# A two-block transformer kernel on one core: VectorE's list in the block-wise inverse, with the work between two levels placed behind the next level's copy

## The chip, the core and the metric

The program runs on one core of a Trainium2 chip. A core has TensorE (matmuls, PE in the profile), VectorE (DVE), ScalarE (ACT), GpSimd (POOL) and SyncE (SP), which issues most of the DMAs. Each engine works through its own list of instructions in the order in which they stand there; they meet only at semaphores. The metric is the device time of one execution, in microseconds (us); lower is better.

## The reference

`first_block` feeds `second_block`. The change lies in the first block's token mixers, in the gated delta rule. For each of 4 tiles of 128 tokens and both directions the kernel needs the inverse of a unit lower triangular matrix of each of 4 heads, and then it carries a state over the tiles:

```python
decay = jnp.exp(jnp.where(incl, gc[..., :, None] - gc[..., None, :], -jnp.inf))
lower = jnp.where(strict, jnp.einsum('bnhid,bnhjd->bnhij', kb, kc) * decay, 0.0)
t_inv = lax.linalg.triangular_solve(eye + lower, ...)
...
def step(s, xs):
    v_new = u_i - jnp.einsum('bhcd,bhde->bhce', w_i, s)
    o_i = ... + jnp.einsum('bhcj,bhje->bhce', qk_i, v_new)
    s = s * gl_i[..., None, None] + jnp.einsum('bhcd,bhce->bhde', kd_i, v_new)
```

Beside it the block computes a neighbourhood attention (softmax over 512 keys, with a bias), a differential attention, a Fourier mix, an output projection, and an expert-choice feed-forward with 16 experts. The second block is another mixer with another set of experts. Everything is float32.

## The kernel before

The whole program is written out by hand: each engine has one function in which every instruction and every semaphore wait stands in the order in which it is to run. Nothing is scheduled by a tool.

**The inverse.** The 4 token tiles (`t` = 0 to 3) follow one another; each takes 6 levels (`lv` = 1 to 6), which double the size of the inverted diagonal blocks. A level is written below as (t, lv). It is a loop over two engines:

1. TensorE, `solve_left` (L1752; at level 6 half the size, L1757): y = lower x inverse, 32 small matmuls.
2. VectorE, the copy of y with a mask into `turned` (L2999; at level 6 L3001).
3. TensorE, `solve_right`: the product p (L1776, at level 6 L1770) and its twin pd (L1783), 32 matmuls each, which read the copy.
4. VectorE, the subtraction of p from `invT` (L3006) and of pd from `inv` (L3011). The next level's `solve_left` reads `invT`, so it waits for the first of the two.

**What is laid between.** Level number n (0 to 23) also carries one step of the attentions. On TensorE, between `solve_left` and `solve_right`: the scores of head-and-tile n (L1649, from n = 8 on L1658), the transposes of n - 1 (L1442) and the values of n - 2 (L1681). On VectorE, behind the copy of y: `attend` (the bias L2813 and the row maximum L2815; from n = 8 on two maxima and no bias), and behind the subtractions `attend_on` (L2825, L2828, L2833). The attentions end with n = 15, that is with (2,4); the levels (2,5) to (3,6) have none, and (3,4) to (3,6) hold a part of the output projection on TensorE (L1828).

**The work between two levels.** At the end of some levels, behind `attend_on`, VectorE does further work of the next token tile, and TensorE's part of it stands behind `solve_right`:

- behind levels 1 and 3 of tiles 0 to 2 `decay_args` (L2841 to L2850), which reads the bank `gb` that `decay_rows` (L1727) filled. ScalarE (`decay_exps`, L2225 to L2233) and GpSimd (L3561, L3563) work on with it.
- behind levels 2 and 4 of tiles 0 to 2 `lower` (L2861, L2863, and from the third tile on L2870, which reads the two banks `qk` of `query_products`, L1718). GpSimd begins the next inverse with it (L3574, L3576).
- at the places named in the table `RECUR` the state updates: `new_state` (L2909, L2912, L2917), which reads a bank `so`, and `new_values` (L2881, L2892), which reads a bank `ws`. TensorE's side is L1808, L1812 and L1793, L1795.
- behind (3,1) `df_sums` (L2925, L2927), behind (3,2) `df_norm` (L2935, L2937, each twice) and `scale_gates` (L2954, twice). TensorE's `mix_turn(2)` behind (3,3) waits for `df_ready`, which `df_norm` sets.

**PSUM.** The class `Banks` deals out the 8 banks of PSUM in turn, in the order of TensorE's list:

```python
def new(self, key):
    while self.turn % 8 in self.held:
        self.turn += 1
    self.turn += 1
    return self.new_on(key, (self.turn - 1) % 8)
```

Before TensorE writes a tile it waits (`free`) until the tile that stands eight places earlier has been read by its reader. A level with differential attention takes 7 banks (y, two scores, transposes, values, p, pd), and the products of `decay_rows`, `query_products` and the state come on top: behind (2,2), for example, 4 banks (two `qk`, `so`, `ws`), so that the bank of the first `qk` comes round again at the values of (2,3), that of the second at p of (2,3), that of `so` at pd and that of `ws` at `gb`.

**Behind the inverse** come the rest of the state updates, the output projection, the router, and the loop over 16 experts, whose weights come by DMA through a ring of buffers; SyncE waits for `mix_ready`, which VectorE sets once the delta rule's output is done, before it issues the loads that fill the ring.

## Time and profile before

| | |
|---|---|
| runs | 2105.51, 2107.21, 2109.47 us; median 2107.21 |
| profiled execution | 2108.91 us, of which the span of its instructions is 2107.0 |
| busy in the span | PE 1699.0 us, DVE 623.2, ACT 280.3, POOL 106.4 |
| the inverse | 176 to 352 us of the span |
| the experts of the first block | from 408 us on |

The span is cut at the first and the last instruction of the profiled execution. The inverse is some 8% of it. "PEclk" is the TensorE clock that was granted: 1.00 is 2.4 GHz, and the level below it is 1.2 GHz; a mean between 0.5 and 1 in a window says how much of the window each level had.

### The profile page before, as it was taken

The page shows a single profiled execution, that of the slowest core. Times are in us where ns is not written, and L with a number is a line of the kernel's source. Part 1 is how long each engine was busy: PE and PEld are TensorE (multiplying, and loading weights), DVE is VectorE, ACT ScalarE, POOL GpSimd, SP SyncE. Part 2 cuts the span into 40 slices and gives each one's busy share as a digit, 9 for nine tenths or more (in the row PEclk, how much of TensorE's full clock was granted, in tenths as well). Part 3 has the DMA queues.
Part 4 walks back from the last instruction along what each step waited for, and adds up shares of the span by engine and source line. Part 5 has one row for each costly group of instructions (what it writes and reads, how often), then busy time and mean ns, then how long its engine had stood idle before and what let it go on. Part 6 is the DMA issues. An engine that isn't in the chain of part 4 may idle for free.

```text
span 2107.0 us, 27246 instructions
## 1 busy us (share of the span) xinstructions
PE 1699.0 (81%) x10986; PEld 877.9 (42%) x10986; DVE 623.2 (30%) x1215; ACT 280.3 (13%) x588; POOL 106.4 (5%) x137
## 2 busy tenths in 40 slices
PE   7999988865666666666555656999999999999997
PEld 3677777511111111111111112888788533333332
DVE  3887654410000000000000001575522522222222
ACT  3213420200000000000000001212420200000001
POOL 0023320100000000000000000010200000000000
PEclk9999989978877787777888787999999999999999
DMA  9861014799999999999999999477247999999996
GB/s 401 357 248 65 3 34 179 308 428 433 429 433 431 430 432 432 430 429 431 434 432 431 430 432 418 161 295 289 95 168 278 397 427 427 426 428 426 428 428 287
DMA packets 55062, 730.56 MB, mean 347 GB/s; under 512 B 6145, under 2 KB 6593, under 8 KB 11330
## 3 DMA queue, kind: packets, MB, share of 16 engines
q1 hardware_dynamic: 52848, 722.23, 81.8%
q10 hardware_dynamic: 2130, 7.14, 1.0%
q8 instruction: 61, 1.00, 0.2%
q14 instruction: 23, 0.19, 0.0%
HBM read 728.26 MB, written 1.09 MB: 346 GB/s over the span
## 4 chain that ended last, share of the span: by engine, by line
PE 48%; DMA 41%; DVE 6%; issue 3%; ACT 1%; POOL 1%; DVEq 0%; SPq 0%; ACTq 0%; POOLq 0%
DMA ring<-in_w_moe 38%; PE psum L938 9%; PE psum L1129 8%; PE psum L978 5%; PE psum L613 4%; PE psum L957 2%; PE psum L631 2%; DMA main<-in_w_moe 2%; PE psum L1279 2%; PE psum L1291 1%; PE psum L1305 1%; PE psum L1828 1%; PE psum L1442 1%; PE psum L913 1%; PE psum L1557 1%
## 5 line engine op out<-in xcount | busy, mean ns | idle before, releaser
L613 PE MATMUL psum<-ring,main 128*32 128x512 f32 x2016 | 333.7, 823 | 189.3 <-DMA ring<-in_w_moe 183.8
L613 PEld LDWEIGHTS psum<-ring,main 128*32 128x32 f32 x2016 | 76.4, 144 | 436.0 <-DMA ring<-in_w_moe 231.5
L631 PE MATMUL psum<-ring,main 128*32 128x512 f32 x1000 | 146.3, 733 | 77.2 <-DMA ring<-in_w_moe 76.5
L673 DVE TENSOR_TENSOR main<-main,psum 128x512 f32<-128x512 f32 x16 | 11.0, 688 | 564.8 <-ACT main L694 564.8
L1129 PE MATMUL psum<-main,ring 128*128 128x256 f32 x768 | 169.2, 382 | 0.0
L938 PE MATMUL psum<-ring,main 128*64 128x512 f32 x688 | 153.8, 595 | 3.9 <-DMA ring<-in_w_moe 3.7
L1129 PEld LDWEIGHTS psum<-main,ring 128*128 128x128 f32 x768 | 146.6, 192 | 20.4 <-issue 0.5
L631 PEld LDWEIGHTS psum<-ring,main 128*32 128x32 f32 x1000 | 33.3, 126 | 174.3 <-DMA ring<-in_w_moe 106.4
L938 PEld LDWEIGHTS psum<-ring,main 128*64 128x64 f32 x688 | 48.7, 137 | 104.0 <-issue 93.0
L676 DVE TENSOR_TENSOR main<-psum,main 128x512 f32<-128x512 f32 x16 | 11.1, 692 | 241.2 <-PE psum L631 241.2
L694 ACT ACTIVATE main<-psum 128x512 f32<-128x512 f32 x16 | 9.6, 597 | 516.4 <-PE psum L613 516.4
L938 PE MATMUL psum<-main 128*64 128x512 f32 x336 | 75.4, 594 | 2.5 <-DMA main<-in_w_moe 2.5
L2163 ACT ACTIVATE main<-psum 128x512 f32<-128x512 f32 (+2 forms) x94 | 44.7, 495 | 206.8 <-PE psum L1129 61.8
L978 PE MATMUL psum<-ring,main 128*64 128x512 f32 x320 | 70.9, 595 | 0.0
L1056 DVE TENSOR_TENSOR main<-main,psum 128x1024 f32<-128x1024 f32 x30 | 36.6, 1221 | 107.9 <-PE psum L957 107.9
L2662 DVE CUSTOM_DVE_ANT_0 ring<-ring,main 128x1024 f32<-128x1024 f32 x48 | 62.0, 1291 | 10.6 <-ACTq L2196 3.5
L957 PE MATMUL psum<-main 128*128 128x512 f32 x120 | 59.5, 618 | 0.0
L3537 POOL TENSOR_SCALAR main<-main 128x1 f32<-128x1 f32 (+4 forms) x13 | 4.0, 306 | 1061.5 <-ACTq L2443 909.5
L2163 ACT ACTIVATE ring<-psum 128x512 f32<-128x512 f32 (+2 forms) x70 | 38.6, 557 | 126.1 <-PE psum L1129 53.7
L1094 ACT ACTIVATE main<-psum 128x512 f32<-128x512 f32 x16 | 9.6, 598 | 342.0 <-PE psum L938 342.0
L2662 DVE CUSTOM_DVE_ANT_0 main<-main,ring 128x1024 f32<-128x1024 f32 x32 | 42.6, 1330 | 31.0 <-DMA main<-in_w_mod_t 27.8
L640 PE MATMUL psum<-main 64*128 64x512 f32 x128 | 39.0, 735 | 14.5 <-DVE main L676 14.5
(511 smaller groups left out, 2054.2 us busy)
## 6 DMA issues: line engine op xcount, KB each, us to landing
ring<-in_w_moe SPq DMA_DIRECT2D x70, 4096.0 KB, 23.7
ring<-in_w_moe SPq DMA_DIRECT2D x105, 2048.0 KB, 22.5
main<-in_w_moe SPq DMA_DIRECT2D x20, 2048.0 KB, 28.6
ring<-in_w_in SPq DMA_DIRECT2D x34, 1024.0 KB, 5.9
main<-in_w_moe SPq DMA_DIRECT2D x33, 1024.0 KB, 19.7
ring<-in_w_mod_t SPq DMA_DIRECT2D x24, 1024.0 KB, 6.9
main<-in_w_mod_t SPq DMA_DIRECT2D x16, 1024.0 KB, 7.3
ring<-in_w_moe SPq DMA_DIRECT2D x13, 1024.0 KB, 12.4
```

The source lines that it names most:

```text
L613: last = mm(psum[32 * j:32 * j + 32, b, :], xg1[:, k, :], w[:, 512 * j:512 * j + 512], start=k == 0, stop=k == KT - 1)
L631: last = mm(psum[q:q + 32, BANK_Y, :], hidT[:, P * (f % 4) + 32 * (f // 4):P * (f % 4) + 32 * (f // 4) + 32], w[:, r, 512 * g:512 * g + 51 ...
L640: last = mm(psum[:, b + g, :], spread[64 * g:64 * g + 64, P * t:P * t + P], ysb[64 * g:64 * g + 64, :], start=True, stop=True)
L913: last = nc.tensor.transpose(psum[:, b + k // 4, P * (k % 4):P * (k % 4) + P], u2[:, t, P * k:P * k + P], onehot2[:, t, :])
L938: last = nc.tensor.matmul(psum[CAP2 * u:CAP2 * u + CAP2, b, :], xg2[:, 4 * h + k, CAP2 * u:CAP2 * u + CAP2], w[u][:, k, :], start=h == 0 a ...
L957: last = nc.tensor.matmul(psum[:, bank + g, :], spread2[:, u, P * t:P * t + P], y2[:, 512 * g:512 * g + 512], start=True, stop=True)
L978: last = nc.tensor.matmul(psum[CAP2 * u:CAP2 * u + CAP2, BANK_Y2 + g, :], hidT2[:, f:f + CAP2], w[u][:, c, 512 * g:512 * g + 512], start=q ...
L1056: nc.vector.tensor_tensor(x[:, t, :], x[:, t, :], psum[:, bank:bank + 2, :].rearrange("p b n -> p (b n)"), ALU.add).then_inc(n_acc, 1)
L1129: last = mm(o[:, 256 * f:256 * f + 256], w[:, k, P * f:P * f + P], uT[:, k, :], start=k == 0, stop=k == KT - 1)
L1279: last = mm(o[:, S * m:S * m + S], w[:, k, :], gr[:, k, :], start=k == 0, stop=k == RT - 1)
L2163: act.activation(dst, src(o), func, scale=scale).then_inc(banks.when_read(key), 1)
L2662: V.tensor_tensor_reduce(w, w, c_rows[b] if late < 0 else c2_row_late, 1.0, M(("b_mod", "b_mod_2")[b])[:, n:n + 1], ALU.mult, ALU.add, mfm ...
```

## The change

VectorE's work between two levels no longer stands at the end of the level (t, lv), but in the following level, behind that level's copy of y and its `attend`, and ahead of its subtraction of p. `scale_gates` moves one level further than the rest (from behind (3,2) to inside (3,4)). On ScalarE `attend` stands ahead of `decay_exps` in levels 2 and 4. No instruction is added or removed, and TensorE's, GpSimd's and SyncE's lists are as before.

```diff
@@ (ScalarE)
                 for lv in range(1, LAST + 1):
+                    attend(n)
                     if t < 3 and lv in (2, 4):
                         decay_exps(t + 1, lv // 2 - 1)
-                    attend(n)
@@ (VectorE)
+            def between_levels(t, lv):
+                if t < 3 and lv in (1, 3):
+                    decay_args(t + 1, lv // 2)
+                if t < 3 and lv in (2, 4):
+                    lower(t + 1, lv // 2 - 1)
+                for kind, step, d, u in RECUR.get((t, lv), ()):
+                    if kind == "so":
+                        new_state(step, d, u)
+                    else:
+                        new_values(step, d, u)
+                if (t, lv) == (3, 1):
+                    df_sums()
+                if (t, lv) == (3, 2):
+                    df_norm()
+                if (t, lv) == (3, 3):
+                    scale_gates()
@@
                     attend(n)
+                    if (t, lv) != (0, 1):
+                        between_levels(*((t, lv - 1) if lv > 1 else (t - 1, LAST)))
                     dve.wait_ge(*banks.full(("p", t, lv)))
@@
                     n += 1
-                    if t < 3 and lv in (1, 3):
-                        decay_args(t + 1, lv // 2)
-                    if t < 3 and lv in (2, 4):
-                        lower(t + 1, lv // 2 - 1)
-                    for kind, step, d, u in RECUR.get((t, lv), ()):
-                        if kind == "so":
-                            new_state(step, d, u)
-                        else:
-                            new_values(step, d, u)
-                    if (t, lv) == (3, 1):
-                        df_sums()
-                    if (t, lv) == (3, 2):
-                        df_norm()
-                        scale_gates()
```

Below are VectorE's rows around the step from (2,2) to (2,3), before. The first row is the last of `attend_on` of (2,2), L2861 to L2870 are `lower` with the two `qk` banks (3 and 4), L2909 and L2881 the state updates with `so` (bank 5) and `ws` (bank 6), L2999 the copy of y of (2,3), L2815 its `attend`, L3006 its subtraction of p.

```order
L2833 SCALAR_TENSOR_TENSOR ring<-ring,main 128x512 [waits bank7_filled,dve_step]
L2861 TENSOR_TENSOR main<-main 128x512 [waits dve_step,decay_masked,bank0_filled,bank2_emptied,bank1_emptied]
L2863 TENSOR_TENSOR main<-main 128x512 [waits dve_step]
L2870 TENSOR_TENSOR ring<-psum,main 128x2x128 [waits dve_step,bank3_filled]
L2870 TENSOR_TENSOR ring<-psum,main 128x2x128 [waits bank4_filled]
L2909 COPY ring<-psum 128x64 [waits bank3_emptied,bank4_emptied,gls_ready,bank5_filled]
L2909 COPY ring<-psum 128x64 [waits dve_step]
L2881 TENSOR_TENSOR ring<-ring,psum 128x256 [waits dve_step,bank6_filled,bank0_emptied]
L2999 TENSOR_TENSOR ring<-psum,main 128x512 [waits dve_step,bank7_filled]
L2815 TENSOR_REDUCE main<-psum 128x1 [waits bank6_emptied,bank0_filled]
L2815 TENSOR_REDUCE main<-psum 128x1 [waits bank1_filled,dve_step]
L3006 TENSOR_TENSOR ring<-ring,psum 128x512 [waits dve_step,bank4_filled]
```

The same piece of VectorE's list in the changed kernel, where the copy of y has the line number L3016 and the subtraction of p L3025.

```order
L2833 SCALAR_TENSOR_TENSOR ring<-ring,main 128x512 [waits bank7_filled,dve_step]
L3016 TENSOR_TENSOR ring<-psum,main 128x512 [waits dve_step,bank7_filled]
L2815 TENSOR_REDUCE main<-psum 128x1 [waits bank6_emptied,bank0_filled]
L2815 TENSOR_REDUCE main<-psum 128x1 [waits bank1_filled,dve_step]
L2861 TENSOR_TENSOR main<-main 128x512 [waits dve_step,decay_masked,bank0_filled,bank2_emptied,bank1_emptied]
L2863 TENSOR_TENSOR main<-main 128x512 [waits dve_step]
L2870 TENSOR_TENSOR ring<-psum,main 128x2x128 [waits dve_step,bank3_filled]
L2870 TENSOR_TENSOR ring<-psum,main 128x2x128 [waits bank4_filled]
L2909 COPY ring<-psum 128x64 [waits bank3_emptied,bank4_emptied,gls_ready,bank5_filled]
L2909 COPY ring<-psum 128x64 [waits dve_step]
L2881 TENSOR_TENSOR ring<-ring,psum 128x256 [waits dve_step,bank6_filled,bank0_emptied]
L3025 TENSOR_TENSOR ring<-ring,psum 128x512 [waits dve_step,bank4_filled]
```

The copy and the two maxima have moved ahead of the seven rows of the work between the levels. TensorE's list at the same place, in (2,3), is the same in both kernels: the scores, the transposes, the values (L1681), p (L1776), pd (L1783), and `decay_rows` (L1727). The "emptied" waits for banks 3, 4, 5 and 6 are those for the tiles that L2870 (twice), L2909 and L2881 read.

```order
L1658 MATMUL psum<-ring,main 128x512 [waits bank1_emptied]
L1442 MATMUL psum<-main,ring 128x128 [waits prob_ready,bank2_emptied]
L1681 MATMUL psum<-main,ring 128x64 [waits bank7_emptied,bank3_emptied]
L1776 MATMUL psum<-ring 64x64 [waits bank2_emptied,bank7_emptied,bank4_emptied]
L1783 MATMUL psum<-ring 64x64 [waits bank5_emptied]
L1727 MATMUL psum<-main 128x128 [waits bank6_emptied]
```

Nothing moved there; only the time at which those banks are read can. The last place is VectorE's list at (3,2), where no attention is left: before, with `new_values` and `df_sums` of the level before ahead of the copy of y (L2999).

```order
L2881 TENSOR_TENSOR ring<-ring,psum 128x256 [waits bank1_filled,bank4_emptied]
L2892 TENSOR_TENSOR ring<-psum,main 128x256 [waits dve_step]
L2925 TENSOR_TENSOR main<-main 128x512 [waits dve_step,bank1_emptied,bank5_emptied]
L2927 TENSOR_REDUCE main<-main 128x8 [waits dve_step]
L2999 TENSOR_TENSOR main<-psum,main 128x512 [waits dve_step,bank3_filled]
L3006 TENSOR_TENSOR main<-main,psum 128x512 [waits bank4_filled]
```

And in the changed kernel, where the copy (L3016) comes first and the four rows stand between it and the subtraction of p (L3025).

```order
L3016 TENSOR_TENSOR main<-psum,main 128x512 [waits bank3_filled,bank0_emptied]
L2881 TENSOR_TENSOR ring<-ring,psum 128x256 [waits bank1_filled,bank4_emptied]
L2892 TENSOR_TENSOR ring<-psum,main 128x256 [waits dve_step]
L2925 TENSOR_TENSOR main<-main 128x512 [waits dve_step,bank1_emptied,bank5_emptied]
L2927 TENSOR_REDUCE main<-main 128x8 [waits dve_step]
L3025 TENSOR_TENSOR main<-main,psum 128x512 [waits dve_step,bank4_filled]
```

What moved is the same as at (2,3): the copy of y is ahead of all of it.

## Rows read from the trace of the kernel before

**Rows 1.** Waits of 176 to 378 us: us in total, times, longest.

```profile
PE psum L1776 <- issue: 14.0, 8, 4.0
```

**Rows 2.** Windows: us, busy and instructions by engine, granted clock, DMA share, GB/s.

```profile
258.00:345.00 87.00, 74.73 (x1264) 65.51 (x1265) 46.95 (x92) 18.29 (x45) 16.39 (x22) 0.88 0.27 105
300.60:309.60 9.00, 9.00 (x116) 8.22 (x113) 1.96 (x4) 1.51 (x3) 2.21 (x4) 0.67 0.01 2
500.00:600.00 100.00, 59.21 (x372) 15.15 (x372) 5.32 (x9) 3.43 (x7) 0.00 (x0) 0.81 1.00 430
```

**Rows 3.** Timeline of (2,1): start, us, engine, line, idle before it.

```profile
257.87 1.15 PE L1752 MATMUL psum<-ring 64*64 64x64 f32 x32
259.07 0.69 DVE L2999 TENSOR_TENSOR ring<-psum,main 128x512 f32<-128x512 f32 x1 [2.51 <-PE psum L1752]
260.11 1.42 DVE L2815 TENSOR_REDUCE main<-psum 128x1 f32<-128x512 f32 x2 [0.35 <-PE psum L1658]
261.43 1.15 PE L1776 MATMUL psum<-ring 64*64 64x64 f32 x32
262.63 0.69 DVE L3006 TENSOR_TENSOR ring<-ring,psum 128x512 f32<-128x512 f32 x1 [1.10 <-PE psum L1776]
```

**Rows 4.** Timeline: (3,4)'s subtraction of p and (3,5)'s start.

```profile
339.01 0.69 DVE L3006 TENSOR_TENSOR main<-main,psum 128x512 f32<-128x512 f32 x1 [3.10 <-PE psum L1776]
339.84 1.15 PE L1752 MATMUL psum<-main 64*64 64x64 f32 x32
```

**Rows 5.** Windows of VectorE alone, cut at each piece between levels.

```profile
182.00:183.55 1.55, 1.44 (x4) 1.00 0.00 0
234.91:236.92 2.01, 1.87 (x5) 1.00 0.00 0
273.88:277.63 3.75, 3.01 (x7) 1.00 0.00 0
284.08:287.64 3.56, 2.85 (x8) 1.00 0.00 0
293.39:296.52 3.13, 2.70 (x6) 0.97 0.01 3
316.18:318.81 2.63, 2.22 (x4) 1.00 1.00 411
324.83:327.95 3.12, 2.69 (x7) 1.00 1.01 420
```

**Rows 6.** Timeline of (0,2): the maximum and the subtraction of p.

```profile
184.76 0.69 DVE L2815 TENSOR_REDUCE main<-psum 128x1 f32<-128x512 f32 x1
185.81 0.69 DVE L3006 TENSOR_TENSOR ring<-ring,psum 128x512 f32<-128x512 f32 x1 [0.36 <-PE psum L1776]
```

**Rows 7.** Timeline of TensorE: the start of p in (1,5).

```profile
246.47 1.09 PE L1776 MATMUL psum<-main 64*64 64x64 f32 x31 [2.19 <-issue]
```

**Rows 8.** Timeline of TensorE, (2,3) to (3,1): starts of y and p.

```profile
273.49 1.15 PE L1752 MATMUL psum<-ring 64*64 64x64 f32 x32
...
278.66 1.53 PE L1776 MATMUL psum<-ring 64*64 64x64 f32 x32 [1.53 <-issue]
...
284.97 1.15 PE L1752 MATMUL psum<-ring 64*64 64x64 f32 x32
...
291.76 1.15 PE L1752 MATMUL psum<-ring 64*64 64x64 f32 x32
...
297.56 1.97 PE L1776 MATMUL psum<-ring 64*64 64x64 f32 x32 [2.81 <-issue]
...
309.66 1.15 PE L1752 MATMUL psum<-main 64*64 64x64 f32 x32
```

**Rows 9.** Timeline of TensorE, (3,2) to (3,4): starts of y and p.

```profile
316.56 1.15 PE L1752 MATMUL psum<-main 64*64 64x64 f32 x32
...
319.74 1.03 PE L1776 MATMUL psum<-main 64*64 64x64 f32 x21 [2.04 <-issue]
...
329.81 1.48 PE L1776 MATMUL psum<-main 64*64 64x64 f32 x32 [4.00 <-issue]
...
333.94 1.15 PE L1752 MATMUL psum<-main 64*64 64x64 f32 x32
```

## The prediction

> **What bounds the kernel now.** I read four views. First the windows: at 500 to 600 us the DMA engines are at 1.00 of their time and move 430 GB/s [rows 2]. The experts' weights bound that part, and the loads that fill the ring wait for the end of the delta rule. So a microsecond that the inverse gains or loses should reach the end of the kernel whole; nothing behind it can make it up or swallow it.
>
> Second the waits of the inverse: TensorE stood idle before p (L1776) 8 times, 14.0 us in all, with no releaser named [rows 1]. Third the timeline, where these idles have a place: 2.19 us in (1,5) [rows 7], 1.53 in (2,3) and 2.81 in (2,5) [rows 8], 2.04 in (3,2) and 4.00 in (3,3) [rows 9]. Each time y is long ready and VectorE is still at the work between the levels, ahead of the copy that p needs. Fourth the granted clock: over 258 to 345 us it is 0.88 [rows 2], so (1 - 0.88) x 2 x 87 = some 21 us of it ran at 1.2 GHz. The 32 matmuls that take 1.15 us at 2.4 GHz [rows 3] take 1.53 and 1.97 behind the idles of 1.53 and 2.81 us [rows 8]; behind the 2.19 they take 1.09 [rows 7]. So the clock fell behind some of these idles and not behind all.
>
> **The rhythm of a level**, with L for the start of y on TensorE and no work between levels [rows 3]: the copy starts at L + 1.20 (259.07 - 257.87), the maxima end at L + 3.66 (261.53), p starts at L + 3.56 (261.43), since TensorE first goes through scores, transposes and values, and the subtraction of p starts at L + 4.76 (262.63). The next y starts 0.83 after that (339.84 - 339.01) [rows 4]. Without attention p needs only the copy: 1.20 + 0.83 = L + 2.03, subtraction at L + 3.23.
>
> Call the length of the work between two levels b [rows 5]: 1.55 us for `decay_args` in tile 0, 2.01 later, 3.75 ahead of (2,3), 3.56 ahead of (2,4), 3.13 ahead of (2,5), 2.63 ahead of (3,2), 3.12 ahead of (3,3). Before, b lies ahead of the copy, where TensorE's scores, transposes and values (3.56 - 1.07 = 2.5 us) cover much of it. After, b starts at L + 3.66 and ends at L + 3.71 + b, against L + 4.76 for p. What is longer than 1.05 us delays the subtraction and so the next level. The change thus swaps one exposure for another. Which is larger depends on the level.
>
> **Levels (0,2) to (0,5): a loss of 1.9 us.** Before, TensorE hardly waits here; the idles are elsewhere. In (0,2) the maximum ends at 185.45 (184.76 + 0.69) and the subtraction starts at 185.81 [rows 6]. After, 1.55 lie between: 185.5 + 1.55 = 187.05, so 1.24 late. (0,3) is 0.25 late on VectorE, but TensorE has `decay_rows` behind pd and covers it: 0. (0,4) and (0,5) lose 0.45 and 0.2 (their b, 1.55 and about 1.45, less the 1.05, and the maximum ends 0.1 earlier with one head's score). Sum 1.9. The bounds: nothing, if the copy's early start were to pay; 6.0, the whole b of four levels, if all were exposed. I take 1.9, since these rows are the level's own.
>
> **Levels (1,2) to (2,2): a gain of 0.25.** Here the idles before p are 14.0 less the four long ones (1.53 + 2.81 + 2.04 + 4.00 = 10.4), so 3.6 us. They go. In return the subtraction comes 2.01 - 1.05 = 1.0 late in three levels and about 1.3 in two (`lower` with its `qk` reads, some 2.3 long); `query_products` and the state products behind pd on TensorE cover 0.6 and all of it in two. Level by level I get +0.25, +0.75, -0.45, -0.2, -0.2 and -0.4. Bounds: -3.6 (only the idles) and +3 (only the exposures).
>
> **Levels (2,3) and (2,4): a loss of 3.85.** This is where the banks matter. Of b = 3.75 the two `qk` reads end 2.0 and 2.35 in, so at L + 5.7 and L + 6.05. The values of (2,3) take the bank of the first: TensorE stands from L + 2.6 to L + 5.7, 3.1 us, and p starts at L + 6.75. Then pd, gb, the state products: the next y at L + 11.4. Before it was 284.97 - 273.49 = 11.48 [rows 8], with the clock at half behind the 1.53. At full clock that is -0.1; but with 3.1 us idle I expect half clock again, which makes values, p and pd about 2 us longer. In (2,4) p waits for `gb`'s bank (L + 4.7), pd for `so`'s (L + 6.6), then `query_products` and the state product: next y at L + 8.65, before 291.76 - 284.97 = 6.79: +1.9. There, before, VectorE had done b while TensorE was still at the state products of (2,3); after, it waits idle for y. Sum -0.1 + 2.0 + 1.9 = 3.8. Bounds: 1.8 with the clock full, 8 with it low through both.
>
> The Trainium skill's "Perfetto Trace Analysis", section "Matmul Optimizations", says that all 8 PSUM banks should be in use to let instructions overlap. They all are here, and the row speaks for the other side of that rule: a bank read later holds up TensorE eight tiles on. Taken alone the rule would give 0 for this term.
>
> **Levels (2,5) and (2,6): a gain of 5.2.** No scores any more. After: copy to L + 1.9, b = 3.13, subtraction at L + 5.05, next y at L + 5.9; TensorE's transposes and values end at 2.7 and p no longer waits. (2,6): at 0.67 granted clock, 2 x 0.33 x 9 = 5.9 us of the 9.0 ran at half [rows 2], of work that is mostly TensorE's; at full clock that is 2.3 us shorter (half of 5.9, less what VectorE does in it), 6.75. Before, the two took 309.66 - 291.76 = 17.9 [rows 8]; after 5.9 + 6.75 = 12.65. Bounds: 3.0 (clock still low), 5.5.
>
> **Levels (3,2) and (3,3): a gain of 5.85.** Copy at L + 1.20, p at L + 2.03; b = 2.63 ends at L + 4.6, subtraction 4.65, next y L + 5.48. In (3,3) b = 3.12 and the gap before it: subtraction at L + 5.2, next y L + 6.03 (`mix_turn(2)` waits for `df_norm` at L + 5.2 and fits). Sum 11.5, before 333.94 - 316.56 = 17.38 [rows 9]. TensorE's idles are then about 1 us each and the clock should stay. Note how it comes about: the subtraction of (3,2) is hardly earlier than before; it is the idle ahead of p, and the half clock behind it, that go. If the clock falls all the same, 1.5 us of each level come back: bound 2.9. `scale_gates` (0.9 us) in (3,4) lies under the 12 matmuls of the projection: nothing. ScalarE's `decay_exps` behind `attend`: its arguments come later than the attention's exp anyway: nothing. GpSimd starts the next inverse 2 to 3 us later, which is needed only behind level 6: nothing; if that cover went, it would cost what `begin_turn` waits.
>
> **Sum:** +1.9 - 0.25 + 3.8 - 5.2 - 5.85 = -5.6 us. The profiled execution (2108.91 us, span 2107.0) is 0.08% above the median; against the median of 2107.21 that gives 2101.6.
>
> **Rivals.** *(a) All falls of the clock go:* the 2.0 in (2,3) falls away, and smaller ones, -7.6 to -9: 2098.5. For it: the idle of 2.19 us without a fall [rows 7]. Against: 1.53 had one [rows 8]. The skill's "TensorE: Matmul & The Clock Gate", Part 1, says that the array's clock halves for want of work and returns with it, between two levels only; those two levels are what the rows show, and by the rule a list with fewer idles should keep the clock. Chance 0.2. *(b) Swap for swap:* the exposures of VectorE are as large as the idles that go, because the clock falls as often, at other places (2.9 us in tile 3, 1 or 2 in (2,4) and (2,5)): between -3 and +2, 2106. For it: VectorE's sum of work is the same, and where it is the bound the order gives nothing. Chance 0.32. *(c) Slower, by the banks:* TensorE's wait for the `qk` bank in (2,3) brings half clock that then holds, since from there on pieces of work and waits alternate. That costs 4 us beyond the 2.0 that I have for (2,3), in (2,3) and (2,4), takes the 2.3 from (2,6) and the 2.9 from (3,2) and (3,3): -5.6 + 4 + 2.3 + 2.9 = +3.6, 2110.8. It decides from the point at which half clock takes some 12 us more than the 21 of before. Chance 0.08. My forecast itself: 0.4.
>
> **The numbers.** From no change 0.2% can be told, 4.2 us. Faster than 2103.0: (a), nearly all of my forecast (its own range 2099.5 to 2104) and a little of (b): 0.58. Within 0.2%: 0.33. Slower: 0.09. The range for 8 in 10 runs from the better end of (a), 2097 (-9 gives 2098.2, and the bounds of the other terms go a little further), to 2108, which takes in (b) but for its last microsecond; what is left out is (c), that microsecond, and about 0.05 below.
>
> **What would show it.** The profile after: the copies of y start 1.2 us behind y everywhere, and TensorE's idle before p falls from 14.0 us to under 5. New idles stand before the values or p of (2,3) and (2,4), about 3 and 1 us, and before y, where it waits for the subtraction. The clock over 258 to 345 us is above 0.92. (0,2) to (0,5) are 1.9 us longer, (2,3) and (2,4) 3.8 longer, (2,5) to (3,3) 11 shorter. The step that I trust least is the clock: if a profile shows it as low as before, the prediction fails towards (b).

## The result and the profile after

The changed kernel took 2110.67 us (median of 20 runs, 2105.95 to 2125.9), the kernel before 2106.34 (20 runs, 2102.2 to 2109.62): ratio 1.0029, 95% interval 1.0020 to 1.0037. This ratio is not the quotient of the two medians, which is 1.0021: the medians lie 4.3 us apart, the means 5.8. So the changed kernel is slower by 4 to 6 us; 2101.6 was predicted, with a range of 2097 to 2108. The profiled execution took 2114.61 us, its span 2112.5.

First TensorE's waits from 176 to 378 us (line, released by: us in total, times, longest), which answer to [rows 1].

```profile
PE psum L1783 <- DVE ring L2870: 3.7, 2, 2.4
PE psum L1681 <- DVE ring L2870: 3.4, 1, 3.4
PE psum L1776 <- issue: 2.2, 3, 0.9
```

The 14.0 us of idle before p with no releaser named are down to 2.2 (two further waits of 1.0 us before p, for the copy of y, are in both kernels, and one of 1.1 for L2843 is new). In their place stand waits for L2870, `lower`'s read of the `qk` banks: 3.4 us before the values of (2,3), 2.4 before pd (L1783) of (1,5), and 1.3 before pd of (1,3). Now the windows that answer to [rows 2], and one of 15 us behind the wait of 2.4 us.

```profile
253.00:268.00 15.00, 15.00 (x144) 12.38 (x138) 7.14 (x15) 3.55 (x8) 4.14 (x7) 0.54 0.00 1
258.00:345.00 87.00, 75.80 (x1249) 65.67 (x1250) 48.62 (x97) 21.73 (x53) 18.05 (x24) 0.89 0.27 104
500.00:600.00 100.00, 55.10 (x372) 14.12 (x376) 5.31 (x9) 3.85 (x9) 0.00 (x0) 0.86 1.00 429
```

The clock over 258 to 345 us is 0.89, before it was 0.88. Forecast was more than 0.92. And 253 to 268, which is (1,6) and was at full clock before, now runs at 0.54. The experts' part is as before, with the DMA engines at 1.00. Next TensorE's timeline: the start of tile 0 (to [rows 6]), pd of (1,3), (1,5) (to [rows 7]), (2,3) to (2,5) (to [rows 8]), (3,1) to (3,4) (to [rows 9]).

```profile
188.60 1.15 PE L1752 MATMUL psum<-ring 64*64 64x64 f32 x32 [1.27 <-DVE ring L3025]
...
235.37 1.15 PE L1783 MATMUL psum<-main 64*64 64x64 f32 x32 [1.30 <-DVE ring L2870]
...
248.94 1.15 PE L1776 MATMUL psum<-main 64*64 64x64 f32 x32 [0.37 <-issue]
252.51 1.15 PE L1783 MATMUL psum<-main 64*64 64x64 f32 x32 [2.43 <-DVE ring L2870]
253.59 0.45 PE L1808 MATMUL psum<-ring 128*64 128x64 f32 x8
253.97 1.06 PE L1757 MATMUL psum<-main 64*64 64x64 f32 x16
254.96 2.08 PE L1658 MATMUL psum<-ring,main 32*128 32x512 f32 x4
...
284.77 1.15 PE L1752 MATMUL psum<-ring 64*64 64x64 f32 x32
290.91 1.35 PE L1681 MATMUL psum<-main,ring 128*128 128x64 f32 x8 [3.35 <-DVE ring L2870]
292.19 1.97 PE L1776 MATMUL psum<-ring 64*64 64x64 f32 x32
298.25 1.15 PE L1752 MATMUL psum<-ring 64*64 64x64 f32 x32
302.99 1.15 PE L1776 MATMUL psum<-ring 64*64 64x64 f32 x32 [1.11 <-DVE main L2843]
305.08 1.84 PE L1783 MATMUL psum<-ring 64*64 64x64 f32 x32 [0.95 <-DVEq L2919]
...
321.37 1.15 PE L1752 MATMUL psum<-main 64*64 64x64 f32 x32
328.26 1.15 PE L1752 MATMUL psum<-main 64*64 64x64 f32 x32
333.75 1.15 PE L1752 MATMUL psum<-main 64*64 64x64 f32 x32
335.81 1.15 PE L1776 MATMUL psum<-main 64*64 64x64 f32 x32 [0.92 <-issue]
339.71 1.15 PE L1752 MATMUL psum<-main 64*64 64x64 f32 x32 [0.21 <-DVE main L3025]
```

Four matmuls of scores (L1658) take 1.13 us at full clock and 2.08 at 254.96. The 32 of p (L1776) take 1.15, and 1.97 at 292.19. So the clock is low behind the 2.43 and behind the 3.35, and again at 305.08. Behind the 2.43 it is not low at once: pd itself still takes 1.15 us, and half clock begins with y of (1,6), at 253.97. Behind the 1.30 of (1,3) there is no fall. From (3,1) on all is at full clock, and the levels are 5.5 and 6.0 us long. The term for (0,2) to (0,5) is seen in the first row: y of (0,3) waits 1.27 us for the subtraction.

From the starts of y each level's length is a difference. In us, grouped as in the prediction (the last two columns are experiments told below, in which TensorE never falls to half clock in the inverse):

| levels | before | changed | difference | predicted | before, filled | changed, filled |
|---|---|---|---|---|---|---|
| (0,2) to (0,5) | 22.77 | 24.83 | +2.1 | +1.9 | 22.78 | 25.28 |
| (1,2) to (2,2) | 53.34 | 61.93 | +8.6 | -0.25 | 53.34 | 55.73 |
| (2,3), (2,4) | 18.27 | 23.86 | +5.6 | +3.8 | 17.41 | 22.02 |
| (2,5), (2,6) | 17.90 | 12.74 | -5.2 | -5.2 | 14.76 | 12.93 |
| (3,2), (3,3) | 17.38 | 11.45 | -5.9 | -5.85 | 15.05 | 11.54 |
| all from (0,2) to (3,6) | 163.84 | 169.11 | +5.3 | -5.6 | 157.53 | 161.76 |

Against this profile of the kernel before, three of the five terms came out to 0.2 us. The miss of 10.9 us lies in (1,2) to (2,2), 8.8, and in (2,3) and (2,4), 1.8. In the first, (1,3) is 1.07 longer (the wait of 1.30 for `lower` of (1,2)), (1,5) 1.3, (1,6) 5.3 and (2,1) 1.3. The column "before" is one execution. The second profile of that kernel (g4, below) has half clock at other places: 57.89, 18.58, 15.73 and 15.81 us in place of 53.34, 18.27, 17.90 and 17.38, in all 164.96. Against it the changed kernel loses 4.0 us in (1,2) to (2,2) and gains 3.0 and 4.4 in the two last groups.

One thing in it is no matter of the clock. VectorE's and GpSimd's timelines of the changed kernel around (1,5):

```profile
245.38 1.51 DVE L2833 SCALAR_TENSOR_TENSOR ring<-ring,main 128x512 f32<-128x512 f32 x1
247.04 0.96 DVE L2883 COPY ring<-ring 128x256 f32<-128x256 f32 x1
248.14 0.69 DVE L3016 TENSOR_TENSOR main<-psum,main 128x512 f32<-128x512 f32 x1
```

```profile
245.25 1.09 POOL L3566 TENSOR_TENSOR main<-main 128x512 f32<-128x512 f32 x1 [8.23 <-ACT main L2227]
246.43 1.42 POOL L3568 TENSOR_TENSOR main<-main 128x512 f32<-128x512 f32 x1
```

And the same two rows of VectorE before:

```profile
241.51 0.75 DVE L2833 SCALAR_TENSOR_TENSOR ring<-ring,main 128x512 f32<-128x512 f32 x1
242.41 0.29 DVE L2883 COPY ring<-ring 128x256 f32<-128x256 f32 x1
```

L2833, the last of `attend_on`, takes 1.51 us in place of 0.75, and the copy behind it 0.96 in place of 0.29, while GpSimd masks the decay terms. The later `decay_args` have put the masks on top of the attention. So the copy of y comes 1.4 us late, and starts 3.8 us behind y, not the 1.2 of the forecast. At (2,3) L2833 takes 1.68, and in (1,6), beside GpSimd's copies (L3591), 1.16.

### The profile page after: what moved, and what is told of

The parts are those of the page before. It is cut to its first block, busy times and chain, and to the rows that moved or that the text cites. A ratio compares the mean times of both kernels' runs of the same rounds, so it can differ in the third digit from the quotient of the medians.

```text
span 2112.5 us, 27248 instructions
## 1 busy us (share of the span) xinstructions
PE 1698.8 (80%) x10986; PEld 877.9 (42%) x10986; DVE 626.2 (30%) x1215; ACT 280.1 (13%) x588; POOL 107.0 (5%) x137
## 3 DMA queue, kind: packets, MB, share of 16 engines
HBM read 728.26 MB, written 1.09 MB: 345 GB/s over the span
## 4 chain that ended last, share of the span: by engine, by line
PE 48%; DMA 41%; DVE 7%; issue 2%; POOL 1%; ACT 1%; DVEq 0%; SPq 0%; ACTq 0%; POOLq 0%
DMA ring<-in_w_moe 38%; PE psum L938 9%; PE psum L1129 8%; PE psum L978 5%; PE psum L613 4%; PE psum L957 2%; PE psum L631 2%; DMA main<-in_w_moe 2%; PE psum L1279 2%; PE psum L1291 1%; PE psum L1828 1%; PE psum L1305 1%; PE psum L913 1%; PE psum L1557 1%; PE psum L1752 1%
## 5 line engine op out<-in xcount | busy, mean ns | idle before, releaser
L613 PE MATMUL psum<-ring,main 128*32 128x512 f32 x2016 | 325.0, 804 | 193.2 <-DMA ring<-in_w_moe 187.7
L631 PE MATMUL psum<-ring,main 128*32 128x512 f32 x1000 | 147.7, 738 | 77.9 <-DMA ring<-in_w_moe 77.9
L676 DVE TENSOR_TENSOR main<-psum,main 128x512 f32<-128x512 f32 x16 | 11.1, 691 | 242.8 <-PE psum L631 242.8
```

The source lines that it names most:

```text
L613: last = mm(psum[32 * j:32 * j + 32, b, :], xg1[:, k, :], w[:, 512 * j:512 * j + 512], start=k == 0, stop=k == KT - 1)
L631: last = mm(psum[q:q + 32, BANK_Y, :], hidT[:, P * (f % 4) + 32 * (f // 4):P * (f % 4) + 32 * (f // 4) + 32], w[:, r, 512 * g:512 * g + 51 ...
```

## The experiments

Each expectation below names its own theories A and B; they change from group to group. In the main A says that a wait of TensorE and the half clock behind it cost the time, with the order of the lists alone worth some 2 us (f1), and B that the order of VectorE's list costs it wherever the clock falls. Most kernels move a part of the work. They hold this in place of the single position, with a set MOVED that names the steps that are late:

```diff
+            def between_levels(t, lv, late):
+                if t < 3 and lv in (1, 3) and (("args", t, lv) in MOVED) == late:
+                    decay_args(t + 1, lv // 2)
+                if t < 3 and lv in (2, 4) and (("lower", t, lv) in MOVED) == late:
+                    lower(t + 1, lv // 2 - 1)
...
                     attend(n)
+                        between_levels(..., True)
...
                     n += 1
+                    between_levels(t, lv, False)
```

ScalarE's `attend` and `decay_exps` go with "args". The ratio is to the kernel before, run on the same chip beside the group's kernels: 2107.06 us for e1, e2, e3 and e7, 2106.31 for e4 and f, 2106.83 for g, 2107.43 for h. As above it is not just the quotient of the medians. "Filled" means matmuls of 256 columns of which nothing is read. Each shows as two in the trace: five of them, x10, take 2.38 us in f2. The sets MOVED are told in words below.

| run | median us (runs) | ratio, 95% interval |
|---|---|---|
| e1_half_back | 2106.98 (12) | 1.0006, 0.9997 to 1.0015 |
| e2_from_25 | 2099.33 (7) | 0.9963, 0.9949 to 0.9976 |
| e3_fill | 2107.51 (12) | 1.0011, 1.0001 to 1.0020 |
| e7_lower14 | 2107.98 (12) | 1.0010, 0.9998 to 1.0022 |
| e4_tile0 | 2109.78 (11) | 1.0015, 1.0005 to 1.0024 |
| f1_after_fill | 2109.10 (11) | 1.0008, 0.9999 to 1.0017 |
| f2_before_fill | 2102.43 (11) | 0.9986, 0.9974 to 0.9998 |
| f3_tail_fill | 2096.65 (5) | 0.9951, 0.9937 to 0.9965 |
| g1_args_back | 2107.68 (12) | 1.0002, 0.9993 to 1.0011 |
| g2_only_args13 | 2105.37 (11) | 0.9995, 0.9985 to 1.0005 |
| h1_lower_back | 2110.18 (12) | 1.0015, 1.0006 to 1.0024 |
| h2_lower14_back | 2108.71 (12) | 1.0006, 0.9997 to 1.0015 |

### Two steps back (e1), and their rescue by filling (e3)

```diff
- MOVED: all
+ MOVED: all but ("args", 1, 3) and ("lower", 1, 4)
```

> The changed kernel, but decay_args behind (1,3) and lower behind (1,4) stand at their old places at the end of those levels. Theory A (TensorE's wait for the bank of the first qk, 2.43 us ahead of pd in (1,5), turned its clock down until (2,1)): no such wait, clock 1.00 over (1,5) to (2,1), and L1752 of (2,1) comes some 10 us earlier than the 268.27 us of the changed kernel; whole time 7 to 8 us below the changed kernel, 2 to 3 below the kernel before. Theory B (the late subtractions of VectorE are the cost, the clock falls somewhere anyway): 1 us at most below the changed kernel.

For e3 the changed kernel gets five filling matmuls between p and pd of (1,5).

```diff
                 last.then_inc(banks.when_full(("p", t, lv)), 1)
+                keep_running(banks.tile(("y", t, lv)), {(1, 5): 5}.get((t, lv), 0))
```

> The changed kernel with 5 matmuls of 256 columns, whose result nobody reads, on TensorE between p and pd of (1,5), where it stood idle for 2.43 us; they take some 2 us and delay nothing. Theory A: the clock stays at 1.00 in (1,6) and (2,1), 6 to 7 us below the changed kernel. Theory B: no difference from the changed kernel.

In e1 (1,5), (1,6) and (2,1) take 8.36, 9.0 and 7.31 us, as before the change. In e3 (1,6) and (2,1) take 8.85 and 7.31, but (1,5) takes 11.10, against 9.65 in the changed kernel. The rows of e3 there, p and the filling:

```profile
252.41 1.90 PE L1778 MATMUL psum<-main 64*64 64x64 f32 x32 [0.38 <-issue]
254.24 3.25 PE L892 MATMUL psum<-main 128*128 128x256 f32 x10
257.42 1.15 PE L1786 MATMUL psum<-main 64*64 64x64 f32 x32
```

The clock was low already at p, behind idles of 0.58 and 0.38 us and before the wait that the filling covers, and was back at pd. So e3 has no fall behind the filled wait, but it has one ahead of it, with no long wait before. The windows of e1 show what took the place of the falls in (1,6) and (2,1).

```profile
190.00:196.00 6.00, 6.00 (x71) 5.62 (x72) 3.20 (x5) 1.58 (x4) 2.30 (x4) 0.51 0.01 3
250.00:275.00 25.00, 21.77 (x367) 18.08 (x366) 16.93 (x34) 9.30 (x23) 6.26 (x10) 1.00 0.01 2
285.00:300.00 15.00, 13.15 (x156) 11.56 (x158) 7.74 (x19) 2.55 (x8) 1.99 (x3) 0.75 0.01 2
```

(1,6) and (2,1) are at 1.00, but (0,3), at 190 to 196, is at 0.51 and 9.71 us long against 6.66 in the changed kernel, whose list there is the same. e3 has that fall too. And (2,3) is 15.05 us long in e1, against 13.48. So e1 cures its place, and the whole gains 4.8 us on the changed kernel by the ratios, not the 7.9 of the three levels nor the 7 to 8 expected; e3 gains 3.8 for 6 to 7 expected.

### Only the late part moved (e2), and tile 0 alone (e4)

```diff
+ MOVED in e2: lower and state updates of (2,4); state updates and df of (3,1), (3,2)
+ MOVED in e4: the four steps of tile 0 (args and lower)
```

> Only the work that falls into (2,5), (3,2), (3,3) and (3,4) is moved: lower and the state update behind (2,4), the sums behind (3,1), norm and gates behind (3,2); everything earlier as before. By my level accounts, which the trace of the changed kernel bore out there (2.85 and 2.3 us gained in (2,5) and (2,6), 2.6 and 3.3 in (3,2) and (3,3)), it is 10 to 11 us faster than the kernel before. Theory B: the clock falls at other places and takes half of it, 5 us. If the change gains nothing anywhere: within 2 us.

> Only the work of token tile 0, behind (0,1) to (0,4), is moved. Both theories: levels (0,2) to (0,5) 2.1 us longer in the trace, as in the changed kernel (1.3, -0.1, 0.5, 0.4). Theory A: in a part of the executions the clock falls in (0,3) as well, behind the new idle of 1.27 us, which costs 3 us there, so that the median is 2 to 4 us above the kernel before. Theory B: 2 us above.

e2 is faster than before, by 0.37%, 7.8 us, between what B (5) and the level accounts (10 to 11) said: (2,5), (2,6), (3,2) and (3,3) take 6.27, 6.73, 5.49 and 5.97 us. e4 is slower, by 0.15%: (0,2) to (0,5) take 24.83, +2.1. These are the prediction's terms, each by itself. But in e2's profile (1,5) and (1,6) are 10.19 and 11.70 us, against 8.36 and 9.0, and there its list is that of before. e4's profile has the same two lengths, at a list that is again that of before, and no fall in (0,3). The start of p in (1,5), in e2:

```profile
246.50 1.97 PE L1777 MATMUL psum<-main 64*64 64x64 f32 x32 [2.19 <-issue]
248.16 2.02 PE L1784 MATMUL psum<-main 64*64 64x64 f32 x32
```

It is the idle of 2.19 us of [rows 7], behind which p took 1.09. In e4 p takes 1.97 behind it too.

### One lower late (e7)

```diff
- MOVED: none (the kernel before)
+ MOVED: only ("lower", 1, 4)
```

> The kernel before with one piece moved: lower behind (1,4) stands behind copy and attend of (1,5). Theory A: TensorE loses its idle of 2.19 us ahead of p and gets one of about 2.2 us ahead of pd, one product later; the clock falls behind it and (1,6) and (2,1) take 5 to 6 us longer. If the fall hangs on more than that one wait (on the longer copy and the stretched L2833 ahead of it), the clock stays and the time is 0 to 1 us below the kernel before. Theory B: within 1 us.

This one step makes (1,6) 14.26 and (2,1) 11.74 us long (before 9.0 and 7.31). TensorE's timeline in e7 and its window:

```profile
248.17 1.15 PE L1784 MATMUL psum<-main 64*64 64x64 f32 x32 [1.86 <-DVE ring L2875]
...
250.58 2.08 PE L1659 MATMUL psum<-ring,main 32*128 32x512 f32 x4
```

```profile
250.00:275.00 25.00, 25.00 (x234) 20.32 (x231) 9.48 (x20) 6.87 (x17) 4.29 (x7) 0.53 0.01 1
```

The wait for the bank is 1.86 us and the clock is low behind it. (1,5) itself is a little shorter, 8.17. The median is only 1 us above before's (by the ratio 2), and the interval includes 1: the twelve runs lie in two groups, seven at 2104 to 2109 and five at 2112 to 2114, and the profiled one (2113.95) is in the upper. So I read the fall here as something that happens in part of the executions; only the one was profiled, so this is not shown.

### TensorE kept busy in its longer waits (f1, f2, f3)

```diff
                 pe.wait_ge(*banks.free(("p", t, lv)))
+                keep_running(o, FILL_P.get((t, lv), 0))
                 pe.wait_ge(*banks.read_out(("y", t, lv)))
```

The same stands ahead of y, of the values and of pd where TensorE waits there. f1 is the changed kernel, f2 the one before, f3 that of e2.

> The changed kernel, with matmuls of 256 columns that nobody reads (some 0.39 us each) wherever its trace shows TensorE idle: ahead of y in (0,3), (0,5), (0,6), (1,5), (2,6), ahead of the values of (2,3), ahead of p in (2,4) and (3,1) to (3,3), ahead of pd in (1,5) and (2,4). Theory A (two halves: the order of the lists alone costs some 2 us, and the falls of the clock, which come by chance at an idle of 1 us or more, cost the rest): the clock stays near 1.00 over 176 to 350 us, 7 to 10 us below the changed kernel, and 1 to 3 us above the kernel before with the same filling. Theory B (the order of VectorE's list is all of the loss): the difference to the kernel before with filling is the 6 us of the unfilled pair, however the clock stands.

> The kernel before, filled in the same way ahead of p: 1 matmul in (1,3) and (1,4), 5 in (1,5), 3 in (2,3), 7 in (2,5), 2 in (3,1), 5 in (3,2), 10 in (3,3), by the idles of its trace. Theory A: no falls, 7 to 9 us below the kernel before. Theory B: no difference.

> The list of e2_from_25 (only the work that falls into (2,5) and later is moved) with the filling of the kernel before ahead of p up to (2,3), and of the changed kernel from (2,6) on. Theory A: a further 2 to 4 us below e2_from_25, 10 to 12 below the kernel before: the moved order in the tail is worth 2 to 4 us at a full clock. Theory B: as e2_from_25.

The windows of f2 and f3 over the stretch of [rows 2]:

```profile
258.00:345.00 87.00, 84.97 (x1392) 72.56 (x1389) 50.89 (x98) 18.32 (x45) 17.78 (x24) 1.00 0.26 105
```

```profile
258.00:345.00 87.00, 83.85 (x1404) 71.26 (x1401) 51.88 (x100) 19.21 (x47) 17.86 (x25) 1.00 0.26 105
```

The clock is 1.00, in f1 too, and in each of the five profiles filled in this way (g1 and g2 below) it is 1.00 over 176 to 352 us. So the last two columns of the table above compare the orders without the clock. The order costs 161.76 - 157.53 = 4.2 us. But in f1 the filling itself adds to this: 1.1 us in (2,4) (four rows of it at 294.59, behind the freeing of the bank), 0.45 in tile 0 (25.28 against 24.83) and 0.23 in (1,5) (9.88 against 9.65). Without these 1.8 us the order costs some 2.5, so 2.5 to 4.2. The half clock costs 163.84 - 157.53 = 6.3 us in the first profile of the kernel before, and in that of the changed one 169.11 - 161.76 = 7.4, or up to 9.1 without the filling's share. In time f1 is 4.6 us above f2 by the ratios; it gained 4.4 on the changed kernel for 7 to 10 expected, and f2 3.0 on the kernel before for 7 to 9. f3 goes from (0,2) to (3,6) in 152.5 us, 5.0 less than f2. It is the fastest kernel here, 0.49% under before (five runs). f1's profile has a fall later, in the products behind the inverse:

```profile
360.00:370.00 10.00, 10.00 (x41) 8.00 (x40) 2.67 (x7) 0.00 (x0) 1.49 (x2) 0.50 0.02 9
```

TensorE is busy there all the time, and g2's profile is at 0.50 in these ten us too. In both unfilled kernels the window from 360 to 370 is at 0.83 or more. What brings that fall none of these runs tells.

### The arguments back, or alone (g1, g2)

```diff
+ g1: f1 with MOVED: all but ("args", 1, 3), ("args", 2, 1)
+ g2: f2 with MOVED: only ("args", 1, 3)
```

> The changed kernel with the filling of f1_after_fill, and with two of the moved steps back at their old place: the decay arguments of (1,3) and (2,1) stand ahead of the next copy of y again, and ScalarE's exponentials of them ahead of its share of attend. Theory A (GpSimd's masks on the arguments run beside VectorE's subtractions of attend_on and lengthen them): every L2833 in Block 1 takes about 0.75 us again (in the changed kernel's profile 1.51 and 1.68 at two places), the level from (1,5) to (1,6) falls from 9.88 to about 8.4 us, that from (2,3) to (2,4) from 11.97 by 0.5 to 1.5, and the time is 1.5 to 3 us under f1_after_fill's. Theory B (the order of VectorE's list alone makes these levels longer, whatever GpSimd does): L2833 may be short, but the two levels keep 9.5 and 11.5 us or more, and the time stays within 1 us of f1_after_fill's.

> The kernel before with the filling of f2_before_fill, and with one step alone moved: the decay arguments of (1,3) behind the copy of y of (1,4), and ScalarE's exponentials behind its share of attend. Theory A: L2833 of (1,5) takes 1.5 us in place of 0.75, and the level from (1,5) to (1,6) goes from 8.36 to 9.2 to 9.9 us; all other levels stay; time +0.8 to +1.5 us to f2_before_fill. Theory B: this one step alone leaves the level at 8.4 to 8.6 us, and the time that of f2_before_fill within 0.5 us.

The rows of L2833 (here L2847) in (1,5), in g1 and in g2:

```profile
246.58 0.75 DVE L2847 SCALAR_TENSOR_TENSOR ring<-ring,main 128x512 f32<-128x512 f32 x1
```

```profile
241.69 1.50 DVE L2847 SCALAR_TENSOR_TENSOR ring<-ring,main 128x512 f32<-128x512 f32 x1
```

All eight are at 0.75 in g1; in g2 the one of (1,5) is at 1.50. The mechanism is there in both directions. In g2 it makes (1,5) 9.58 us and (1,6) 9.26, 1.4 together over f2, and the whole inverse 1.3 longer; its ratio is 0.0009 over f2's, within the intervals. In g1 (1,5) goes from 9.88 to 8.89, but (1,4) rises by 0.56 and (2,2) by 0.42, and (2,3) stays at 11.82. In all g1 is 0.4 us shorter than f1: at (2,3) theory A was wrong, the bank sets that level, not the masks. So the masks' price in the changed kernel is between 0.4 and 1.3 us, by the traces alone.

### Both kernels once more (g3, g4)

No edit: a second profile of each.

> The changed kernel, unchanged, for a second profile. Theory A (TensorE's clock falls behind idle times of more than about 1 us, but not at every one and not in every execution): outside the falls the levels have the lengths of the first profile within 0.1 us ((0,2) to (0,5) 6.07, 6.66, 6.06, 6.04; L2833 of 1.5 us in (1,5)), and at least one of the stretches that ran at half clock there ((1,6) and (2,1); (2,3); (2,4)) runs at full clock, or another falls. Theory B (the falls belong to the order of the lists): the same three stretches are at half clock, 14.3, 8.6, 13.5 and 10.4 us long.

> The kernel before, unchanged, for a second profile. Theory A: the falls do not all lie where they did in the first ((2,3), (3,1) and (3,2)); one idle time behind which the clock stayed up there, such as that of 2.2 us ahead of the p of (1,5), may have a fall behind it here, and without a fall the levels have the lengths of the filled kernel within 0.1 us. Theory B: the same stretches, the same lengths.

The changed kernel repeats its levels within 0.1 us, 169.17 us in all, the falls included: there theory A was wrong, and in two profiles of two the fall behind the wait for pd is there. The kernel before does not repeat. TensorE's timeline of (1,5) and the window in its second profile:

```profile
247.38 1.87 PE L1776 MATMUL psum<-main 64*64 64x64 f32 x31 [2.19 <-issue]
...
252.67 2.08 PE L1658 MATMUL psum<-ring,main 32*128 32x512 f32 x4
```

```profile
250.00:275.00 25.00, 24.72 (x330) 20.01 (x330) 14.15 (x31) 9.31 (x24) 4.29 (x7) 0.80 0.00 1
```

One kernel, one idle of 2.19 us: p at 1.09 us in one execution [rows 7] and at 1.87 in the other. (1,5) and (1,6) are 1.8 and 2.7 longer, while (2,5) and (2,6) are 2.2 shorter; in all 164.96 us against 163.84. With e2 and e4 that makes three profiles of four in which this piece of list falls behind the 2.19 us. The fourth is the one that the prediction was worked out from. Between the second profiles the change costs 169.17 - 164.96 = 4.2 us, where the first had 5.3.

### Only lower back (h1, h2)

```diff
+ h1: MOVED: all but ("lower", 1, 2), ("lower", 1, 4), ("lower", 2, 2)
+ h2: MOVED: all but ("lower", 1, 4)
```

> The changed kernel, without filling, with one kind of moved step back: lower of (1,2), (1,4) and (2,2), whose reads free the qk banks, stand ahead of the next copy of y again; everything else stays moved. Theory A (the late reads of the qk banks make TensorE stand 2.43 us before pd of (1,5) and 3.35 us before the values of (2,3), and the clock falls behind these waits): both waits go, (1,6) and (2,1) take about 9.0 and 7.3 us again in place of 14.3 and 8.6, (2,3) about 10 to 11.5 in place of 13.48, and the time is 5 to 9 us below the changed kernel's, so at or under that of before: ratio 0.9965 to 1.000. Theory B (the clock falls somewhere whatever the order, and the longer lists of VectorE cost the rest): the waits go, but half clock turns up at other idle times, and the ratio stays at 1.001 to 1.003.

> The changed kernel, without filling, with lower of (1,4) alone back at its old place. Theory A: the wait of 2.43 us before pd of (1,5) goes; (1,6) and (2,1) take 9.0 and 7.3 us (14.3 and 8.6 in the changed kernel's two profiles), (1,5) stays at 9.2 to 9.7 because GpSimd's masks still lengthen L2833 to 1.5 us there; the time is 4 to 6.5 us below the changed kernel's: ratio 0.9995 to 1.001. Theory B: (1,6) and (2,1) are short, but another stretch that was at full clock falls, and the ratio stays at 1.002 or more.

h2 gains what theory A said for it: 1.0006 against 1.0029. (1,6) and (2,1) take 8.79 and 7.31. But (1,5) takes 11.15, not the 9.2 to 9.7 expected, since p waits again and the clock falls behind that:

```profile
251.85 1.83 PE L1777 MATMUL psum<-main 64*64 64x64 f32 x32 [3.01 <-issue]
```

h1 was expected at or under before and is at 1.0015. The wait for pd is gone, that for the values, expected gone, is still 2.1 us, and idles before p are back, 7.6 us in four. (1,3) and (1,5) fall to half clock, with 11.03 and 11.49 us, and (2,3) still takes 13.56. Taking the waits for the bank away made others, as theory B had it.

## Why the prediction was wrong

**What held.** The idle before p went, as forecast (14.0 to 2.2 us). Tile 0 lost 2.1 us (1.9), confirmed by e4. (2,5) to (3,3), without (3,1), gained 11.1 (11.05), and e2, with that part alone, is 0.37% faster. The agreement of the 11.1 is in part luck: 5.8 of it is half clock that this one profile of before had there, and against g4 the gain is 7.4. The time reached the end whole: (3,6) starts 5.9 us later and the execution took 5.7 longer.

**The step that failed: "Levels (1,2) to (2,2): a gain of 0.25".** It measured +8.6 (+4.0 against g4, and +2.2 at full clock). It counted only how late VectorE's work makes the subtraction of p; pd stands in it as cover, and the banks were not followed. But `lower` of (1,4) reads the bank that pd of (1,5) takes over, and `lower` of (1,2) that of pd of (1,3). I had followed that chain at (2,3) and not here, four and six levels earlier. In (1,5) TensorE stands 2.43 us, and behind it (1,6) runs at half clock and (2,1) in part (granted clock 0.50 and 0.83): 22.9 us against 16.4 filled, 6.5 us. In e7's profile this step alone makes the wait and the fall. e1 and h2, which put it back, have no fall in (1,6) and (2,1); nor has e3, where the clock was low ahead of the wait and came back during the filling. A further 2.4 us are there at full clock (0.2 of it the filling's): 1.1 is the wait in (1,3), and 0.2 to 1.3 (g1, g2) the masks beside L2833. The prediction had no term for them; it put the later exponentials at "nothing" and did not ask what GpSimd's share would run beside. The upper bound of the term, +3, had no half clock in it. The list of its level figures also has six for seven levels.

**Levels (2,3) and (2,4): mis-sized.** +5.6 for +3.8 (the heading of that term says 3.85; its sum is 3.8). The wait for the `qk` bank is there (3.35 us for 3.1) with half clock behind it: (2,3) is +2.0, as forecast. (2,4) is +3.6 for +1.9: its waits at p and pd are where they were forecast (L + 4.7, and L + 6.8 for 6.6), but pd runs at half clock (1.84 us for 32 matmuls). I had ended the fall with (2,3). The sentence that the Trainium skill's rule ("Perfetto Trace Analysis", section "Matmul Optimizations", all 8 banks in use) gives 0 here is settled by the trace: all eight are in use and the term is +5.6.

**The clock.** The sum booked the end of the half clock in (2,5) to (3,3) as a gain that stays, and had none new but the 2.0 in (2,3). The filled pairs show the bill: before, 6.3 us of the inverse hang on half clock, after 7.4 to 9.1. What went from (2,5) to (3,3) came up in (1,6), (2,1), (2,3) and (2,4). At full clock the tail's gain is 1.8 + 3.5 = 5.3 and the losses in front are 2.5 + 2.4 + 4.6, less the filling's 1.8. So at full clock too the change is slower, where -5.6 was forecast. My rival (c) has nearly the measured time (2110.8), in part by luck: its wait for the `qk` bank with half clock behind it came, four levels earlier too, but the tail kept its gain, and half clock did not hold on there. The prediction's own sign, a clock as low as before (0.89 for 0.88), points at (b), swap for swap; the order adds a loss of 2.5 to 4.2 us that (b) did not have.

**What stays open.** Why the same idle is followed by a fall in one execution and not in another. Whether the changed kernel falls in (1,6) in all its runs: both its profiled executions (2114.6 and 2114.3 us) are 3.9 and 3.7 us above its median, and 14 of its 20 runs were below both, so in many runs some of the falls may be absent. How much of the time the fall in (1,6) costs over all runs: e7, which has it in its profile, is only 0.10% above the kernel before, with an interval from -0.02 to 0.22. Which idles bring a fall: e3 has one behind 0.58 and 0.38 us, and the changed kernel none behind 1.30. What brings the fall at 358 to 380 us.

## What to carry to other kernels

Where banks (or any buffers) rotate, moving a read later moves it past every tile that will claim its bank: follow each moved read forward to its claimant, at all the places, before pricing the copy that it makes way for. Don't book the end of a half-clock stretch seen in one profile as a gain unless the change ends TensorE's waits as a whole; price the order at full clock (from rows at full clock), and give the clock as a spread. And take a reordering apart: here, at full clock, the same move is worth -5 us in (2,5) to (3,3), where TensorE has no scores, and some +8 in the levels before them, and the part alone (e2, f3) beats both kernels.

## What the hardware showed beyond that

The same idle of 2.19 us of TensorE before the same matmuls was followed by half clock in three profiles (e2, e4, g4) and not in a fourth (before), and two of the four are of one kernel. The Trainium skill's "TensorE: Matmul & The Clock Gate", Part 1, says that the grid on which the chip judges activity runs freely and does not start with the kernel; by that rule the same idle can count in one execution and not in the next. The trace agrees so far as it differs between executions; no run here shows the grid, and the changed kernel's two profiles did not differ. Unread matmuls in TensorE's waits kept the granted clock at 1.00 over the whole inverse in five profiles of five and made the kernel before faster by 0.14% (0.02 to 0.26), though f1 and g2 had a fall to 0.50 behind it, at 360 to 370 us.

A VectorE instruction with two inputs in SBUF took 1.50 to 1.69 us in place of 0.75 at (1,5) and (2,3), and a copy 0.96 in place of 0.29, beside GpSimd's multiplications, and GpSimd's second took 1.42 in place of 1.09. Started 0.13 us behind the first of GpSimd (1.09 us), L2833 ended 0.55 us after that was over. The Trainium skill's "SBUF — State Buffer", section "🔬 SBUF: two separate sides", says that the two engines share a pair of ports as an exclusive lock, held for the whole instruction, for a VectorE operation with two SBUF inputs against a GpSimd one that reads SBUF; by that rule L2833 would wait the rest of GpSimd's instruction, 0.96 us, and then run 0.75, in all 1.71. The trace has 1.51. At (2,3) GpSimd's instruction (1.27 us) starts 0.13 us ahead, so the rule gives 1.14 + 0.75 = 1.89, and the trace has 1.68. So L2833 ends 0.55 and 0.54 us behind GpSimd's instruction, where the rule has 0.75: the trace agrees in what waits for what, and lies 0.2 us under the rule's time at both places. No run here shows why.
